# A recurrent layer's gate tiles moved behind its recurrences' inputs, its scans a tile ahead, its output in two halves, and two pairs of first tiles in turn

## The chip, the cores and the metric

The kernel runs on one NeuronCore of a Trainium2 chip. The metric is the device time of one execution in microseconds, as the median of several runs. All numbers of the profile come from one profiled execution; engines are named as the profile names them: PE (TensorE matmuls), PEld (its weight loads), DVE (VectorE), ACT (ScalarE), POOL (GpSimd), SP (SyncE).

## What is computed

Two blocks follow each other over one sequence of 512 tokens with 1024 features, all in fp32. The first block is a modulated mixer (state-space part and attention in parallel) and a feed-forward layer of 4096 features, `x + gate2 * (relu(h2 @ w_mlp1)**2 @ w_mlp2)`. The second block is a gated recurrent layer, then a causal latent attention with a gate, then a last norm. The change is in the recurrent layer and at two borders of stages:

```python
def rglru_layer(x, norm_g, w_in, conv_w, conv_b, w_rg, b_rg, w_ig, b_ig, lam, w_out):
    u = rms_norm_2(x, norm_g) @ w_in                 # w_in is 1024 x 2560
    xb, gate = u[..., :1280], u[..., 1280:]
    xb = causal_depthwise_conv(xb, conv_w, conv_b)   # width 4
    r = sigmoid(xblk @ w_rg + b_rg)                  # ten blocks of 128 x 128
    i = sigmoid(xblk @ w_ig + b_ig)
    log_a = -8.0 * r * softplus(-lam)
    a = exp(log_a)
    bterm = sqrt(-expm1(2.0 * log_a)) * (i * xb)
    _, hs = associative_scan(_lin_combine, (a, bterm), axis=1)
    return (hs * silu(gate)) @ w_out                 # w_out is 1280 x 1024
```

Its result is added to the stream x. The layer after it begins with two norms of the new x and projects it into the key-value and query latents.

## The kernel before

Activations lie with features on the 128 partitions and the 512 tokens along the free axis, so the stream is KT = 8 tiles of 128x512 (`x_stream`). Every big product is made in "feature tiles" of 128 output features: `feature_tile` (L1045) goes over blocks k of 128 input features, and each block takes three matmuls (`split_mm`, L1039, so L1041 to L1043), high times high, high times low, low times high, since every fp32 operand is split into a high and a low part. A tile over 1024 inputs is therefore 24 matmuls of 512 columns, the recurrent layer's output tile over 1280 inputs is 30.

The weights come as one stream in the order in which PE uses them, cut into slabs of four 128x128 blocks (256 KB). For each slab SP issues a load into a ring of four raw buffers, ACT writes the high part (`hi_upto`, L592 to L600, into a ring of seven), POOL subtracts to get the low part (`low`, L554), and PE waits for the low part (`weights`, L1031). ACT makes no slab by itself: `tile_in(name)` (L602) first converts up to six slabs (AHEAD) past the slab where the tile begins, and a slab's buffer is free when PE has done the last tile of the slab seven before. Since ACT's queue runs strictly in order, an ACT that waits for DVE converts nothing in the meantime.

`plan` (L105) writes down the order of all tiles by hand, and with it the order of the weights; `BANK_OF` (L196 to L205) gives each tile its PSUM bank in turn from a ring of banks that depends on the tile's kind, and `start` (L1023) lets PE wait until the bank's last tile has been read out ("evacuated").

The recurrent layer has RT = 10 tiles of 128 channels. `rnn_steps` (L87) gives the order that all engines follow. An "xb" tile n is the convolution's input: DVE scales it by the norm's factor in PSUM (`scale_tile`, L1949), ACT writes the first tap with the bias (`conv_first`, L846, the activation is L851), DVE adds three taps (L1972), ACT writes its high part (`conv_hi`, L858), and DVE the low part (L1985), the latter only after it has scaled the next xb tile. "gates" n, two steps later, is two tiles of three matmuls each ("rg" and "ig"), three tanhs and one exp on ACT (L866, L870, L873, L876) and two combining instructions on DVE (`gate_x`, L1989, and `decay`, L1996). After the gates of tiles 4 and 9 a detour works on five tiles at once: DVE's `halve` (L2023, with L1959 and L1965) and ACT's `roots` (L878, square roots L883) alternate, with a table load on ACT before the roots and one before the next tanh. A "gt" tile n is the gate: `scale_tile`, then `recurrence` (L1998: one tensor_scalar that adds 1 to the decay, L2000, and the scan, L2002), then `gate_y` (L2004), which needs ACT's tanh of the gate (L890), then ACT's `gate_hi` (L892, L895) and DVE's `y_low` (L2012, L2020). In the order of before, gt tiles 0 to 4 stand between the xb and gates tiles of steps 7 to 11, and gt tiles 5 to 9 follow at the end.

Then come eight output tiles "oa" of ten blocks each (L1356). DVE adds each to the stream (`add_to_stream`, L2050, the instruction is L2052), ACT writes the high part of the next input, DVE its low part.

Two other places are touched. The first matrix of the feed-forward layer ("m1", L1340) starts when the norm of the stream is written block by block (`norm_split`, L1547, low parts L1554). The last projection ("ob", L1492) starts while the last attention head is still being finished on DVE and ACT (L2201 to L2206, L978, `split_head`, L2171).

In the latent attention, the first gate tile ("gh", 0) is read out late by DVE (`gate2`, L2166, after `rope_key`); the four value tiles ("vh", 0, 0 to 3) follow it on PE, and their banks come from a ring of three (0, 1, 2).

## Time and profile before

| | us |
|---|---|
| median of 3 runs | 1716.84 |
| lowest, highest | 1707.63, 1719.45 |
| the profiled execution's own time | 1715.92 |
| its span in the profile | 1713.8 |
| PE busy | 1618.2 (94%) |
| DVE busy | 1013.9 (59%) |
| POOL busy | 774.3 (45%) |
| ACT busy | 738.9 (43%) |

The profiled execution took 2.1 us more than its span. Matmul records overlap: a record of 0.39 us stands for a matmul that starts 0.23 us after the last one, so the distance of two starts is what a matmul costs, and busy time is no measure of it. The granted clock over the whole span was 0.978.

### The profile page before, as it was taken

The page shows a single profiled execution, that of the slowest core. Times are in us where ns is not written, and L with a number is a line of the kernel's source. Part 1 is how long each engine was busy: PE and PEld are TensorE (multiplying, and loading weights), DVE is VectorE, ACT ScalarE, POOL GpSimd, SP SyncE. Part 2 cuts the span into 40 slices and gives each one's busy share as a digit, 9 for nine tenths or more (in the row PEclk, how much of TensorE's full clock was granted, in tenths as well). Part 3 has the DMA queues.
Part 4 walks back from the last instruction along what each step waited for, and adds up shares of the span by engine and source line. Part 5 has one row for each costly group of instructions (what it writes and reads, how often), then busy time and mean ns, then how long its engine had stood idle before and what let it go on. Part 6 is the DMA issues. An engine that isn't in the chain of part 4 may idle for free. (4 is left out here: it accounts for less than half of the span.)

```text
span 1713.8 us, 23817 instructions
## 1 busy us (share of the span) xinstructions
PE 1618.2 (94%) x8328; PEld 1335.5 (78%) x8328; DVE 1013.9 (59%) x1357; ACT 738.9 (43%) x1347; POOL 774.3 (45%) x546
## 2 busy tenths in 40 slices
PE   4899999999999899999989999999999699789987
PEld 4687888888878688887868888888888587667766
DVE  4778989888739698487241311112488813357662
ACT  2366656646633544323242333334476434323332
POOL 1235565656656510256634444445535354233423
PEclk9999999999999999999999999999999899889998
DMA  7233343434332200367423333333323233111212
GB/s 300 66 114 111 117 136 108 115 123 123 105 87 67 68 26 1 123 234 245 137 72 99 98 99 93 101 90 98 90 76 93 75 92 98 50 49 50 62 32 74
DMA packets 76245, 171.30 MB, mean 100 GB/s; under 512 B 8240, under 2 KB 8624, under 8 KB 72816
## 3 DMA queue, kind: packets, MB, share of 16 engines
q1 hardware_dynamic: 68832, 133.09, 26.6%
q10 hardware_dynamic: 7312, 36.83, 6.2%
q8 instruction: 67, 1.10, 0.3%
q14 instruction: 34, 0.28, 0.1%
HBM read 167.67 MB, written 2.23 MB: 99 GB/s over the span
## 5 line engine op out<-in xcount | busy, mean ns | idle before, releaser
L557 POOL TENSOR_TENSOR w_lo<-w_raw,w_hi 128x512 fp32r<-128x512 f32 x457 | 683.5, 1517 | 691.6 <-ACT w_hi L599 691.2
L1041 PE MATMUL bank<-a_hi,w_hi 128*128 128x512 f32 x1040 | 418.3, 402 | 18.2 <-DVE a_lo L1554 8.9
L1043 PE MATMUL bank<-a_hi,w_lo 128*128 128x512 f32 x1040 | 408.7, 393 | 0.0
L1042 PE MATMUL bank<-a_lo,w_hi 128*128 128x512 f32 x1040 | 408.5, 393 | 0.0
L599 ACT ACTIVATE w_hi<-w_raw 128x512 fp32r<-128x512 f32 x457 | 261.3, 619 | 147.4 <-PE bank L1043 123.7
L1041 PEld LDWEIGHTS bank<-a_hi,w_hi 128*128 128x128 f32 x1040 | 197.2, 190 | 69.8 <-issue 15.7
L1041 PE MATMUL bank<-b_hi,w_hi 128*128 128x512 f32 x600 | 237.7, 396 | 0.6 <-POOL w_lo L557 0.6
L1043 PE MATMUL bank<-b_hi,w_lo 128*128 128x512 f32 x600 | 235.8, 393 | 0.0
L1042 PE MATMUL bank<-b_lo,w_hi 128*128 128x512 f32 x600 | 235.8, 393 | 0.0
L1043 PEld LDWEIGHTS bank<-a_hi,w_lo 128*128 128x128 f32 x1040 | 197.3, 190 | 42.6
L1042 PEld LDWEIGHTS bank<-a_lo,w_hi 128*128 128x128 f32 x1040 | 197.5, 190 | 41.3 <-issue 1.9
L1041 PEld LDWEIGHTS bank<-b_hi,w_hi 128*128 128x128 f32 x600 | 114.2, 190 | 24.7 <-POOL w_lo L557 1.1
L1043 PEld LDWEIGHTS bank<-b_hi,w_lo 128*128 128x128 f32 x600 | 114.1, 190 | 24.5
L1042 PEld LDWEIGHTS bank<-b_lo,w_hi 128*128 128x128 f32 x600 | 114.1, 190 | 23.8
L1939 DVE SCALAR_TENSOR_TENSOR x_stream<-bank,small,x_stream 128x512 f32<-128x512 f32 x32 | 24.0, 750 | 140.4 <-PE bank L1043 140.4
L1932 DVE TENSOR_TENSOR tmp<-tmp 128x512 f32<-128x512 f32 x32 | 22.7, 708 | 123.6 <-ACT tmp L831 123.6
L697 ACT ACTIVATE M<-cs_rows,cs 128x128 f32<-128x128 f32 x256 | 78.0, 388 | 0.0
L1615 DVE SCALAR_TENSOR_TENSOR tmp<-bank,small,tmp 128x510 f32<-128x510 f32 (+1 forms) x96 | 71.9, 749 | 3.4
L511 POOL TENSOR_TENSOR square_sum<-square_sum,sq 128x512 f32<-128x512 f32 x31 | 40.1, 1294 | 63.5 <-ACT sq L611 63.5
L1530 DVE SCALAR_TENSOR_TENSOR ada_acc<-ada_piece,small,ada_acc 128x2048 f32<-128x2048 f32 x21 | 62.2, 2962 | 7.6 <-DMA ada_piece<-ada 6.2
L831 ACT ACTIVATE tmp<-bank 128x512 f32<-128x512 f32 x32 | 19.1, 598 | 101.3 <-PE bank L1043 101.3
L1262 PEld LDWEIGHTS bank<-v_and_ones,probs 128*128 128x128 f32 x512 | 60.2, 192 | 1.9 <-ACT gates_early L644 1.2
(327 smaller groups left out, 2460.9 us busy)
## 6 DMA issues: line engine op xcount, KB each, us to landing
w_raw<-ws SPq DMA_DIRECT2D x457, 256.0 KB, 2.7
cs_rows<-cs_scratch ACTq DMA_DIRECT2D x16, 1024.0 KB, 5.2
ada_piece<-ada ACTq DMA_DIRECT2D x16, 1024.0 KB, 5.3
ada_piece<-ada SPq DMA_DIRECT2D x8, 1024.0 KB, 15.0
x_stream<-x SPq DMA_DIRECT2D x1, 2048.0 KB, 15.9
x_stream<-x ACTq DMA_DIRECT2D x1, 2048.0 KB, 9.1
out<-x_stream SPq DMA_DIRECT2D x8, 256.0 KB, 2.1
rope_table<-rope ACTq DMA_DIRECT2D x1, 512.0 KB, 3.4
```

The costliest lines, as they stand in the source:

```text
L511: nc.gpsimd.tensor_tensor(sq_sum[:, :], first[:, :], sq[n % 2][:, :], ALU.add).then_inc(sq_added, 1)
L557: nc.gpsimd.tensor_tensor(wlo[b][:, :], raw[n % RAW_RING][:, :], r32(whi[b][:, :]), ALU.subtract)\
L599: A(whi[n % RING][:, :], raw[n % RAW_RING][:, :], ACT.Copy).then_inc(hi_done, 1)
L697: a(A(Dm[:, r, w], csB[:, r, w], ACT.Abs, bias=csT[:, c, h:h + 1]))
L1041: mm(out, lh, rh, start=first, stop=False)
L1042: mm(out, lh, rl, start=False, stop=False)
L1043: return mm(out, ll, rh, start=False, stop=last)
L1262: ins = mm(OQ[h % 2][:, i * W:(i + 1) * W], PT[:, c, i * P:(i + 1) * P], vv[:, c, h // 4, :], start=(c == 0 and i == 0), stop=(c == NCH - ...
L1530: V.scalar_tensor_tensor(into[:, :], src[:, :], csl[:, k:k + 1], into[:, :], ALU.mult, ALU.add).then_inc(ada_acc, 1)
L1615: ins = V.scalar_tensor_tensor(out[:, o], src[:, s], cwh[:, j * 24 + i:j * 24 + i + 1], out[:, o], ALU.mult, ALU.add)
L1932: v(V.tensor_tensor(full[:, :], r[:, :], r[:, :], ALU.mult))
L1939: inc_evac(V.scalar_tensor_tensor(xF[:, m, :], gb(name)[:, :], modc[:, 5 * KT + m:5 * KT + m + 1], xF[:, m, :], ALU.mult, ALU.add), name)
```

## The change

1. In `rnn_steps` all ten gt tiles stand behind the last gates tile; before, five of them stood between the xb and gates tiles. The weights' order follows.
2. DVE's addition of 1 to the decay goes to ACT: after each five square roots ACT runs five Identity activations with bias 1 (`a_full`).
3. The scan of tile n + 1 is issued before `gate_y(n)`, and writes over its own input; `y_low(n - 1)` is issued after `scale_tile` of tile n instead of right behind `gate_y(n - 1)`.
4. Each output tile is made in two halves of five blocks: first the first half of all eight tiles, each added to the stream, then the second half of all eight.
5. The first two tiles of m1 and of ob are made in turn, block by block (`tile_pair`), so that each arriving block feeds six matmuls instead of three.
6. The sixteen half tiles instead of eight shift all later banks; ("gh", 0) is restricted to banks 0 and 1.

```diff
@@ rnn_steps
     for n in range(RT + RNN_LAG):
-        if n >= RNN_HALF + RNN_LAG:
-            steps.append(("gt", n - RNN_HALF - RNN_LAG))
         if n < RT:
             steps.append(("xb", n))
         if n >= RNN_LAG:
             steps.append(("gates", n - RNN_LAG))
-    return steps + [("gt", n) for n in range(RT - RNN_HALF, RT)]
+    return steps + [("gt", n) for n in range(RT)]
@@ plan
-    for m in range(KT):
-        tile(("oa", m), RT)
+    for part in range(2):
+        for m in range(KT):
+            tile(("oa", part, m), RNN_HALF)
@@ banks
-        (0, 1, 2) if _name[0] in LATENT else (0, 1, 3, 5, 6) if _name[0] == "ob" else (0, 1, 3, 4, 5, 6)
+        (0, 1) if _name == ("gh", 0) else (0, 1, 2) if _name[0] in LATENT else (0, 1, 3, 5, 6) if _name[0] == "ob" else (0, 1, 3, 4, 5, 6)
@@ ScalarE
-            def roots(first):
-                for n in range(first, first + RNN_HALF):
+            def roots(first, count):
+                for n in range(first, first + count):
                     act.wait_ge(p_ready, n + 1)
                     if n >= 2:
                         act.wait_ge(xbs_done, n - 1)
                     A(root_v[n % 2][:, :], t[n % 2][:, :], ACT.Sqrt, scale=-0.25).then_inc(s_done, 1)
+                for n in range(first, first + count):
+                    A(t2[:, n, :], t2[:, n, :], ACT.Identity, bias=ones[:, 0:1]).then_inc(a_full, 1)
...
             for m in range(KT):
-                hi_upto(slab_of(("oa", m)) + AHEAD)
-                wait_evac(act, ("oa", m))
+                hi_upto(slab_of(("oa", 0, m)) + AHEAD)
+            for m in range(KT):
+                hi_upto(slab_of(("oa", 1, m)) + AHEAD)
+                wait_evac(act, ("oa", 1, m))
@@ TensorE
+            def tile_pair(names, hi, lo, ready):
+                for name in names:
+                    start(name)
+                blocks = TILES[names[0]][2]
+                for k, parts in enumerate(zip(*(weights(name) for name in names))):
+                    pe.wait_ge(*ready(k))
+                    for name, (b, o) in zip(names, parts):
+                        ins = split_mm(gb(name)[:, :], whi[b][:, o:o + P], wlo[b][:, o:o + P], hi(k), lo(k), k == 0,
+                                       k == blocks - 1)
+                        if k == blocks - 1:
+                            ins.then_inc(gemm_done, 1)
...
             for f in range(FQ):
-                for m in range(KT):
-                    feature_tile(("m1", f, m), in_a, in_a_lo, (rdyA, KT))
+                if f == 0:
+                    tile_pair((("m1", 0, 0), ("m1", 0, 1)), in_a, in_a_lo, lambda k: (rdyA, KT + k + 1))
+                for m in range(0 if f else 2, KT):
+                    feature_tile(("m1", f, m), in_a, in_a_lo)
...
-            for m in range(KT):
-                feature_tile(("oa", m), lambda k: bH[:, k, :] if k < KT else yH[k - KT][:, :],
-                             lambda k: bL[:, k, :] if k < KT else yL[k - KT][:, :],
-                             lambda k: (rdyB, 24 + KT * FQ + k + 1) if k < KT else (rdyY, k - KT + 1))
-                if m:
-                    stat("nkv", m - 1)
+            for part in range(2):
+                k0 = part * RNN_HALF
+                for m in range(KT):
+                    feature_tile(("oa", part, m), lambda k: in_y(k0 + k), lambda k: in_y_lo(k0 + k),
+                                 lambda k: (rdyB, 24 + KT * FQ + k0 + k + 1) if k0 + k < KT else (rdyY, k0 + k - KT + 1))
...
-            for m in range(KT):
-                feature_tile(("ob", m), in_a, in_a_lo, (rdyA, 4 * KT))
-                if m:
-                    stat("fin", m - 1)
+            tile_pair((("ob", 0), ("ob", 1)), in_a, in_a_lo, lambda k: (rdyA, 4 * KT + k + 1))
+            for m in range(2, KT):
+                feature_tile(("ob", m), in_a, in_a_lo)
+                stat("fin", m - 1)
@@ VectorE
             def recurrence(n):
                 ve.wait_ge(xbs_done, n + 1)
-                v(V.tensor_scalar(t2[:, n, :], t2[:, n, :], 1.0, None, ALU.add))
-                v.settle()
-                v(V.tensor_tensor_scan(scan[:, :], t2[:, n, :], xbi[:, n, :], 0.0, ALU.mult, ALU.add))
+                ve.wait_ge(a_full, n + 1)
+                v(V.tensor_tensor_scan(xbi[:, n, :], t2[:, n, :], xbi[:, n, :], 0.0, ALU.mult, ALU.add))
...
                 else:
+                    if n == 0:
+                        recurrence(n)
                     scale_tile(("gt", n), rstd, gt_scaled)
-                    recurrence(n)
+                    if n:
+                        y_low(n - 1)
+                    if n + 1 < RT:
+                        recurrence(n + 1)
                     gate_y(n)
-                    y_low(n)
+            y_low(RT - 1)
...
             for m in range(KT):
-                add_to_stream(("oa", m), m)
+                add_to_stream(("oa", 0, m), m)
+            for m in range(KT):
+                if m < 2:
+                    wait_evac(ve, ("oa", 0, m))
+                add_to_stream(("oa", 1, m), m)
                 if m:
-                    wait_evac(ve, ("oa", m - 1))
+                    wait_evac(ve, ("oa", 1, m - 1))
                     gain_low("nkv", m - 1, aL, aH, hiA, 3 * KT, rdyA)
```

## Rows read from the trace of the kernel before

**Rows 1.** stretch table: busy us (instructions) PE, PEld, DVE, ACT, POOL, then PEclk, DMA, GB/s

```profile
1340.00:1370.00 30.00, 20.44 (x76) 15.03 (x75) 23.91 (x27) 11.09 (x20) 13.33 (x10) 0.84 0.27 72
```

**Rows 2.** waits of PE: releaser: us in total, times, longest

```profile
PE bank L1041 <- DVE a_lo L1554: 8.9, 9, 3.1
PE bank L1041 <- DVE y_lo L2020: 7.5, 2, 5.3
PE bank L1041 <- POOL w_lo L557: 7.5, 6, 4.5
```

**Rows 3.** timeline of PE: start us, us, line, operation [idle before <- releaser]

```profile
1217.35 0.39 PE L1041 MATMUL bank<-a_hi,w_hi 128*128 128x512 f32 x1
...
1314.96 0.40 PE L1041 MATMUL bank<-xb_hi,w_hi 128*128 128x512 f32 x1
...
1337.57 0.47 PE L1041 MATMUL bank<-a_hi,w_hi 128*128 128x512 f32 x1 [4.46 <-POOL w_lo L557]
...
1352.13 0.39 PE L1041 MATMUL bank<-b_hi,w_hi 128*128 128x512 f32 x1
...
1367.17 0.80 PE L1041 MATMUL bank<-y_hi,w_hi 128*128 128x512 f32 x1 [5.31 <-DVE y_lo L2020]
```

**Rows 4.** timeline of DVE, same columns, the recurrent stage and its end

```profile
1276.54 0.69 DVE L1953 TENSOR_TENSOR bank<-bank,rstd 128x512 f32<-128x512 f32 x1
...
1337.74 1.22 DVE L2002 TENSOR_TENSOR_SCAN std<-tanh_half_log_a,gated_x 128x512 f32<-128x512 f32 x1
...
1341.01 0.69 DVE L2020 SCALAR_TENSOR_TENSOR b_lo<-y_full,b_hi 128x512 fp32r<-128x512 f32 x1 [0.69 <-ACT b_hi L895]
1341.73 0.70 DVE L1953 TENSOR_TENSOR bank<-bank,rstd 128x512 f32<-128x512 f32 x1
...
1343.17 2.20 DVE L2002 TENSOR_TENSOR_SCAN std<-tanh_half_log_a,gated_x 128x512 f32<-128x512 f32 x1
...
1348.10 0.70 DVE L1953 TENSOR_TENSOR bank<-bank,rstd 128x512 f32<-128x512 f32 x1
...
1418.82 0.69 DVE L2052 TENSOR_TENSOR x_stream<-x_stream,bank 128x512 f32<-128x512 f32 x1 [5.53 <-PE bank L1043]
```

**Rows 5.** timeline of ACT, same columns, the recurrent stage

```profile
1269.43 1.28 ACT L883 ACT_TABLE_LOAD   x1
...
1282.85 0.78 ACT L851 ACTIVATE xb_conv<-bank,params 128x512 f32<-128x512 f32 x1 [0.50 <-PE bank L1043]
...
1328.17 0.81 ACT L876 ACTIVATE tmp<-tmp,small 128x512 f32<-128x512 f32 x1
```

**Rows 6.** groups of instructions, 1217.3 to 1418.9 us: busy us, mean ns | idle before

```profile
L599 ACT ACTIVATE w_hi<-w_raw 128x512 fp32r<-128x512 f32 x64 | 36.5, 617 | 0.0
...
L1972 DVE SCALAR_TENSOR_TENSOR xb_conv<-bank,params,xb_conv 128x509 f32<-128x509 f32 (+2 forms) x30 | 22.4, 747 | 2.6 <-ACT xb_conv L851 1.9
...
L1989 DVE SCALAR_TENSOR_TENSOR gated_x<-tmp,xb_conv 128x512 f32<-128x512 f32 x10 | 12.0, 1198 | 4.1 <-ACT tmp L870 4.1
...
L873 ACT ACTIVATE tanh_half_log_a<-tmp,small 128x512 f32<-128x512 f32 x10 | 8.1, 814 | 0.0
...
L866 ACT ACTIVATE tmp<-bank,small 128x512 f32<-128x512 f32 x10 | 6.8, 677 | 0.0
```

**Rows 7.** timeline of PE at the starts of m1 and of ob

```profile
864.35 0.77 PE L1041 MATMUL bank<-a_hi,w_hi 128*128 128x512 f32 x1 [2.47 <-DVE a_lo L1554]
...
874.62 0.40 PE L1041 MATMUL bank<-a_hi,w_hi 128*128 128x512 f32 x1
...
880.07 0.39 PE L1041 MATMUL bank<-a_hi,w_hi 128*128 128x512 f32 x1
...
1655.44 0.69 PE L1041 MATMUL bank<-a_hi,w_hi 128*128 128x512 f32 x1
...
1662.29 0.50 PE L1041 MATMUL bank<-a_hi,w_hi 128*128 128x512 f32 x1 [1.58 <-DVE a_lo L2171]
```

**Rows 8.** timeline of PE at the third value tile

```profile
1483.50 0.80 PE L1041 MATMUL bank<-w_hi,ckv_hi 128*128 128x512 f32 x1 [7.29 <-DVE tmp L2166]
```

More of the change, by code:

```diff
@@ L36 @@
 RNN_HALF = RT // 2
+ROOTS_AT = {RNN_HALF - 1: (0, RNN_HALF), RT - 1: (RNN_HALF, RT - RNN_HALF)}
 CKT, CQT = KV_RANK // P, Q_RANK // P
@@ L361, in build @@
             sil = [sb(f"gate_silu{b}", [P, SEQ]) for b in range(2)]
-            scan, yF = std, sb("y_full", [P, SEQ])
+            yF = sb("y_full", [P, SEQ])
         with Arena():
@@ L425, in build @@
         xb_scaled, gt_scaled = sem("xb_scaled"), sem("gt_scaled")
-        p_ready, a_exp, am1_done = sem("decay_variance"), sem("decay"), sem("decay_minus_one")
+        p_ready, a_exp, am1_done, a_full = (sem(n) for n in ("decay_variance", "decay", "decay_minus_one", "decay_full"))
         g_th, y2_ready = sem("gate_tanh"), sem("y2_ready")
@@ L518, in _ @@
                 for m in range(1, POOLED[norm]):
-                    tile = (kind, FQ - 1, m) if kind == "m2" else (kind, m)
+                    tile = (kind, FQ - 1, m) if kind == "m2" else (kind, 1, m) if kind == "oa" else (kind, m)
                     squares.setdefault(min((TILES[tile][1] + TILES[tile][2] - 1) // BPS + RING, N_SLABS), []).append((norm, m))
@@ L906, in _ @@
                         conv_hi(n + RNN_LAG)
-                    if n % RNN_HALF == RNN_HALF - 1:
-                        roots(n + 1 - RNN_HALF)
+                    if n in ROOTS_AT:
+                        roots(*ROOTS_AT[n])
                 else:
@@ L1355, in _, with in_y, in_y_lo @@
                     feature_tile((kind, n), in_a, in_a_lo)
-            for m in range(KT):
-                feature_tile(("oa", m), lambda k: bH[:, k, :] if k < KT else yH[k - KT][:, :],
-                             lambda k: bL[:, k, :] if k < KT else yL[k - KT][:, :],
-                             lambda k: (rdyB, 24 + KT * FQ + k + 1) if k < KT else (rdyY, k - KT + 1))
-                if m:
-                    stat("nkv", m - 1)
+            def in_y(k):
+                return bH[:, k, :] if k < KT else yH[k - KT][:, :]
+            def in_y_lo(k):
+                return bL[:, k, :] if k < KT else yL[k - KT][:, :]
+            for part in range(2):
[3 more added lines that the diff above has]
+                                 lambda k: (rdyB, 24 + KT * FQ + k0 + k + 1) if k0 + k < KT else (rdyY, k0 + k - KT + 1))
             pe.wait_ge(rows_kept, 2)
@@ L2009, in gate_y @@
                 v.settle()
-                V.tensor_tensor(yF[:, :], scan[:, :], th[:, :], ALU.mult).then_inc(y2_ready, 1)
+                V.tensor_tensor(yF[:, :], xbi[:, n, :], th[:, :], ALU.mult).then_inc(y2_ready, 1)
             def y_low(n):
@@ L2021, in y_low, with scale_inputs @@
                 ve.wait_ge(rdy, r0 + 1)
-            def halve(first):
+            def scale_inputs(first, count):
                 variance(first)
                 variance(first + 1)
-                for n in range(first, first + RNN_HALF):
+                for n in range(first, first + count):
                     scale_x(n)
-                    if n + 2 < first + RNN_HALF:
+                    if n + 2 < first + count:
                         variance(n + 2)
@@ L2041, in _ @@
                         conv_low(RT - 1)
-                    if n % RNN_HALF == RNN_HALF - 1:
-                        halve(n + 1 - RNN_HALF)
-                else:
+                    if n in ROOTS_AT:
+                        scale_inputs(*ROOTS_AT[n])
+                else:
+                    if n == 0:
+                        recurrence(n)
                     scale_tile(("gt", n), rstd, gt_scaled)
-                    recurrence(n)
+                    if n:
+                        y_low(n - 1)
+                    if n + 1 < RT:
+                        recurrence(n + 1)
                     gate_y(n)
-                    y_low(n)
+            y_low(RT - 1)
             def add_to_stream(name, m):
```

4 lines of the change are left out of this document (2 added, 2 removed).

## The prediction

> **What bounds the kernel now.** I read the page first: PE is busy 94% of the span, so a gain can only be time in which PE stands still or runs at the lower clock. Then the waits of PE: the three lines that the change can touch are 8.9 us on low parts of a norm, 7.5 on the recurrent layer's last low parts and 7.5 on weights [rows 2]. Then PE's timeline for the price of work: a tile of 24 matmuls takes 880.07 - 874.62 = 5.45 us, 0.227 a matmul [rows 7]. With it the recurrent stage splits into three stretches [rows 3]:
>
> - xb, gates and five gt tiles, 1217.35 to 1316.3 (the last gates tile starts at 1314.96 and takes 1.4): 99.0 us for 420 matmuls, which cost 95.3. The other 3.7 are mostly the small matmuls of the norm.
> - the five last gt tiles, to 1352.13: 35.8 us for 120 matmuls (27.2). 8.6 are lost, 4.46 of it in one wait for weights: ACT had not yet turned to converting.
> - the output, to 1418.8 (DVE's last addition starts there [rows 4]): 66.7 us for 240 matmuls (54.5). 12.2 are lost, 5.31 of it in one wait for the low part of y.
>
> So PE runs ahead of an ACT/DVE chain: PE has made gates 9 at 1316.3, ACT ends its exp at 1329.0 [rows 5]. A stall also costs clock: from 1340 to 1370 the granted clock is 0.84, between the levels 1.2 and 2.4 GHz [rows 1]. 16% of 30 us is 4.8 us, idle time included; I take 1.6 us for one long stall.
>
> **1. Stretch without gt tiles.** For PE 300 matmuls remain: 68.1 + 3.7 us, so it could start gt 0 at 1289.2. The chain decides otherwise. Up to the five-tile detour behind gates 4 nothing changes; DVE comes out of it at 1276.5 [rows 4], ACT 0.7 earlier, at 1275.8. New there: five Identity activations. The trace has none in this place; the bounds are the 0.57 us of a slab conversion (36.5 / 64) and the 0.81 of a tanh with a bias [rows 6]; I take 0.66, nearer to the conversion since the source is also in SBUF: 3.3 us (2.9 to 4.1), on the path. Then conv_first 7 starts at 1279.1 instead of 1282.85 [rows 5], because gt 0 no longer stands in front of it. One step of the chain: conv_first 0.7, two slabs 1.1, three tanhs and an exp, whose records of 0.68 and 0.81 overlap by 0.1, 2.6, DVE's decay 0.7, the next scaling 0.6 [rows 6], some 0.2 for handovers: 5.9 us, against 6.8 on PE (30 matmuls). The first step also takes the table load for tanh, 1.28 [rows 5]: 7.2. So conv_first 9 comes at 1292.2, the low part that gates 9 needs one step later, at 1298.1, and gates 9 is done at 1299.5, with some slow matmuls 1300.0. PE stands for 10.8 us that it did not stand before (between 0 and 15: that is the chain hidden wholly, or each step 1.4 longer). DVE's additions of 1 (L2000) leave the chain, but were in it only with the gt tiles.
>
> **2. Gate tiles.** At gates 9 ACT has converted six slabs ahead, which is gt 0 to 2: 16.3 us, to 1316.3. ACT ends the exp of gates 9 about 3.3 us after PE, at 1303.3; the detour takes the same 7.1 us as the first one (1269.43 to 1276.54 [rows 4, 5]), its roots end at 1309.7, the five Identities at 1313.0. The next slab is there with its low part 2.0 later, at 1315.0: no stall, with 1.3 us to spare. A second table load and tanh 0 (1.9), then DVE's two gate instructions (0.69 each, as the additions [rows 4]): y 0 is ready at 1317.0, and the two slabs behind it at 1319.6 and later, where PE wants the first at 1319.0: 0.6 us of stall.
> From there one tile costs DVE and ACT now 1348.10 - 1341.73 = 6.37 us [rows 4], more than PE's 5.45, and this is why PE ran dry. Two things leave this cycle: L2000 (1343.17 - 1341.73 - 0.61 for the scaling = 0.83) and the wait of y_low for ACT, 0.69 [rows 4], since the next scaling covers it; the tanh is covered by the scan ahead. 4.84 remain, under 5.45, so PE sets the pace. Gate tiles end at 1300.0 + 54.5 + 0.6 + 1.6 of clock = 1356.7.
>
> **3. Output.** y 9 follows within some 4 us and is wanted first by the second half, 8 x 15 matmuls (27.2 us) later. No wait is left: 240 matmuls at 0.229 (tile borders) are 55.0, to 1411.7. The halves add eight additions to DVE, 8 x 0.69 = 5.5 us, under PE: DVE idles 5.53 between two of them [rows 4], and a half tile takes 3.4; without that cover they would cost 5.5. ACT's conversions of the first half are all queued before its first waiting copy, so no slab hangs on DVE. POOL's sum of squares comes at twice the pace; I take 0 for it (up to 1.3, one sum at the end, below nothing excluded).
> Gain of the stage: 1418.8 - 1411.7 = 7.1.
>
> **4. First tiles in turn.** m1: blocks arrive every 1.45 us; the first tile took 864.35 to 874.62, the second ended at 880.07 [rows 7]. Six matmuls are 1.36 us, about the arrival's pace, and the first few run slow: 864.35 + 8 x 1.36 + 1.6 = 876.8. Gain 3.2 (0 if its weights are late; 4.9 if only the last block bounds it). Four slabs are needed at once; nothing holds ACT and POOL from having made six before the norm. ob: the last block was waited for at 1662.29 [rows 7], two tiles would end at 1668.4. In turn it is wanted at 1655.44 + 42 x 0.227 = 1665, when it is there: end 1666.6, gain 1.8 (0 to 1.8).
>
> **5. Banks.** PE waits 7.29 us for DVE to read out the first latent gate [rows 8]. This is the third value tile, since it takes gh 0's bank. Counting the new bank list, gh 0 sits in bank 1 and the second value tile takes it: the same release, six more matmuls behind it. 1.4 us at full clock, 2.6 at the lower one; I take 2.0 lost. The other latent tiles keep their distance of three in the ring.
>
> **Sum.** 7.1 + 3.2 + 1.8 - 2.0 = 10.1 us. The profiled execution took 1715.92, so 1705.8; the median of before, 1716.84, is only 0.9 above it.
>
> **Rivals.**
> A: the chain is hidden, PE reaches gt 0 at its own pace. For it: a step of the chain, 5.9, is shorter than PE's 6.8. Against: the chain starts the race at 1279.1, when xb 7, by PE's pace from 1264, is already some 8 us old. Then 1289.2 + 54.5 + 55.0 = 1398.7, 20.1 gained, with the rest 23.1: 1692.8.
> B: weights starve the gate tiles, slower than before. ACT converts two slabs only after each y, so PE follows the DVE/ACT cycle wherever that is over 5.45. Evidence: the scan took 2.20 us in one tile and 1.22 in another [rows 4], gated_x 1.20 in the mean [rows 6] where an instruction of its size takes 0.75, so DVE is sometimes held up. If the reordering saves nothing and y_low doubles, the cycle is 7.07; with y 0 2.4 us later, y 9 is at 1383.0, the slab of the fifth half tile 2.6 later, 15 slabs (40.8) and the clock behind it: 1428.0, 9.2 lost, in sum 6.2 slower: 1722.1. It turns the gain of the whole into a loss from a cycle of about 6.4.
> The Trainium skill, "SBUF — State Buffer", section "Who interferes with whom", says that a VectorE instruction with two SBUF inputs contends with a GpSimd one that reads SBUF, and that the loser is blocked for the whole instruction. By that rule y_low, the scan and the product are all exposed to POOL's low parts, which is B's mechanism; the trace agrees for the scan, with 2.20 against 1.22.
> C: the pairs do nothing, since their second tiles' weights are late. For it: 7.5 us of waits for weights exist [rows 2]; against: none stands at these two places. 5.0 less gain: 1710.8.
>
> **How the numbers follow.** Forecast 0.70, A 0.15, B 0.07, C 0.08. A measurement of this kernel tells about 1% (17 us) from no change. My 10.1 us are 0.6%: "same". Faster by over 1% needs 17.2 us: A, and a tail of the forecast (a chain 7 us shorter than I think), 0.18 together. Slower by over 1% needs more than B: 0.04. The range goes from A's time less 1.8 to near B's: 1691 to 1720.
>
> **What would show it.** Right: gt 0 starts on PE near 1300; a gap of some 10 us before it, in two or three waits for xb_lo (L1985), which were none; no wait of over 1 us among the gate tiles; the 4.46 and 5.31 waits gone; a step from gate tile to gate tile of 5.45 on PE; the stage ends near 1411.7 counted from an unchanged start, less the 3.2 of m1; the wait at the value tile is at the second one. Wrong: PE waits for w_lo among the gate tiles (B), or no wait before gates 9 (A), or waits for w_lo in the pairs (C).

## The result, and the profile after

The changed kernel takes 1704.1 us (median of 10 runs, 1698.4 to 1710.9), the kernel before 1716.9 in the runs beside it: ratio 0.9933, 95% interval 0.9912 to 0.9955. The prediction was 1705.8.

The profiled execution was the longest of the ten, 1710.9 us with a span of 1709.0. Cut at six places, the two spans compare so:

| stretch of the span, us | before | after | difference | predicted |
|---|---|---|---|---|
| to the first matmul of m1 | 864.35 | 870.09 | +5.7 | 0 |
| from there to the first xb matmul | 353.00 | 350.61 | -2.4 | -3.2 |
| recurrent stage: to the start of DVE's last addition to the stream | 201.47 | 193.30 | -8.2 | -7.1 |
| to the first latent score | 84.19 | 84.49 | +0.3 | +2.0 |
| to the first ob matmul | 152.43 | 154.55 | +2.1 | 0 |
| to the end | 58.36 | 55.96 | -2.4 | -1.8 |

The first line holds no changed instruction; in the twelve experiments below it took 863.6 to 867.7 us. The fifth took 151.4 to 152.8 in eight of them and 154.5 to 155.4 in the other four. So 7.8 us of this execution lie where nothing of the change is seen at work; without them it would be 1703.1, close to the median.

PE's waits in the stage, in its timeline (start, duration, line, operation, [idle before <- releaser]). They answer to [rows 3]:

```profile
1220.70 0.39 PE L1044 MATMUL bank<-a_hi,w_hi 128*128 128x512 f32 x1
...
1281.31 0.47 PE L1044 MATMUL bank<-xb_hi,w_hi 128*128 128x512 f32 x1 [0.58 <-DVE xb_lo L2009]
...
1285.31 0.50 PE L1044 MATMUL bank<-a_hi,w_hi 128*128 128x512 f32 x1 [2.37 <-DVE xb_conv L1996]
...
1295.94 0.77 PE L1044 MATMUL bank<-xb_hi,w_hi 128*128 128x512 f32 x1 [3.29 <-DVE xb_lo L2009]
...
1301.21 0.76 PE L1044 MATMUL bank<-xb_hi,w_hi 128*128 128x512 f32 x1 [2.37 <-DVE xb_lo L2009]
...
1303.91 0.63 PE L1044 MATMUL bank<-a_hi,w_hi 128*128 128x512 f32 x1
...
1358.95 0.39 PE L1044 MATMUL bank<-b_hi,w_hi 128*128 128x512 f32 x1
```

All idle time now stands before the last gates tile: four waits, 8.6 us. The gate tiles (1303.9 to 1358.95, ten of 5.5 us) and the output run without one. The waits of 4.46 and 5.31 us of before are gone. PE's waits over the whole span (us in total, times, longest), beside [rows 2]:

```profile
PE bank L1044 <- DVE tmp L2198: 10.6, 1, 10.6
PE bank L1044 <- DVE a_lo L1578: 7.1, 5, 3.2
PE bank L1044 <- DVE xb_lo L2009: 6.2, 3, 3.3
...
PE bank L1044 <- DVE xb_conv L1996: 2.4, 1, 2.4
...
PE bank L1044 <- POOL w_lo L556: 0.5, 1, 0.5
```

The waits for a norm's low parts fell from nine to five (8.9 to 7.1 us), those for weights from 7.5 to 0.5, those for y's low parts from 7.5 to none. One wait grew: 10.6 us at the value tiles, where it was 7.3 [rows 8].

ACT's timeline around the two detours, beside [rows 5]; x5 is five instructions in one record:

```profile
1279.08 3.16 ACT L884 ACTIVATE tanh_half_log_a<-tanh_half_log_a,consts 128x512 f32<-128x512 f32 x5
1282.14 0.76 ACT L850 ACTIVATE xb_conv<-bank,params 128x512 f32<-128x512 f32 x1
...
1312.68 3.16 ACT L884 ACTIVATE tanh_half_log_a<-tanh_half_log_a,consts 128x512 f32<-128x512 f32 x5
1315.75 0.62 ACT L598 ACTIVATE w_hi<-w_raw 128x512 fp32r<-128x512 f32 x1
```

Five additions of 1 take 3.16 us, and conv_first of xb 7 starts right behind them; in the second detour the next slab does. DVE's timeline over one gate tile, beside [rows 4], and POOL's two conversions in it:

```profile
1319.64 0.69 DVE L1977 TENSOR_TENSOR bank<-bank,rstd 128x512 f32<-128x512 f32 x1
1320.42 0.69 DVE L2043 SCALAR_TENSOR_TENSOR b_lo<-y_full,b_hi 128x512 fp32r<-128x512 f32 x1
1321.15 2.21 DVE L2025 TENSOR_TENSOR_SCAN gated_x<-tanh_half_log_a,gated_x 128x512 f32<-128x512 f32 x1
1323.29 0.66 DVE L2030 SCALAR_TENSOR_TENSOR gate_silu<-gate_silu,bank 128x512 f32<-128x512 f32 x1
1323.98 1.02 DVE L2033 TENSOR_TENSOR y_full<-gated_x,gate_silu 128x512 f32<-128x512 f32 x1
1324.92 0.69 DVE L1977 TENSOR_TENSOR bank<-bank,rstd 128x512 f32<-128x512 f32 x1
```

```profile
1320.99 1.29 POOL L556 TENSOR_TENSOR w_lo<-w_raw,w_hi 128x512 fp32r<-128x512 f32 x1 [3.26 <-ACT w_hi L598]
1322.24 2.20 POOL L556 TENSOR_TENSOR w_lo<-w_raw,w_hi 128x512 fp32r<-128x512 f32 x1
```

From scaling to scaling 5.28 us, without a gap that names a releaser. Before it was 6.37. The two engines stretch each other: the scan takes 2.21 us here and 1.22 alone, and POOL's second subtraction 2.20 where the first takes 1.29.

The pairs on PE, beside [rows 7], and the value tile, beside [rows 8]:

```profile
870.09 0.76 PE L1044 MATMUL bank<-a_hi,w_hi 128*128 128x512 f32 x1 [2.48 <-DVE a_lo L1578]
...
875.26 0.39 PE L1044 MATMUL bank<-a_hi,w_hi 128*128 128x512 f32 x1
...
883.42 0.39 PE L1044 MATMUL bank<-a_hi,w_hi 128*128 128x512 f32 x1
...
1477.59 0.80 PE L1044 MATMUL bank<-w_hi,ckv_hi 128*128 128x512 f32 x1 [10.56 <-DVE tmp L2198]
...
1498.49 0.30 PE L1448 MATMUL bank<-knope_hi,qnope_hi 128*128 128x128 f32 x1 [3.14 <-DVE qnope_lo L2176]
...
1653.04 0.69 PE L1044 MATMUL bank<-a_hi,w_hi 128*128 128x512 f32 x1
```

The third tile of m1 starts 13.3 us after the first instead of 15.7, with no wait inside; the first twelve matmuls, to 875.26, go at 0.43 us each, so at the lower clock of 1.2 GHz.

### The profile page after: what moved, and what is told of

Its sections match the earlier page's. It is cut to its first block, busy times and chain, and to the rows that moved or that the text cites. A ratio compares the mean times of both kernels' runs of the same rounds, so it can differ in the third digit from the quotient of the medians.

```text
span 1709.0 us, 23860 instructions
## 1 busy us (share of the span) xinstructions
PE 1620.6 (95%) x8328; PEld 1341.9 (79%) x8328; DVE 1024.2 (60%) x1355; ACT 744.7 (44%) x1357; POOL 780.5 (46%) x546
## 4 chain that ended last, share of the span: by engine, by line
PE 80%; DVE 14%; ACT 3%; issue 2%; DMA 1%; SPq 0%; ACTq 0%; DVEq 0%; POOL 0%
PE bank L1044 21%; PE bank L1046 21%; PE bank L1045 21%; PE bank L1279 3%; DVE ada_acc L1554 2%; PE bank L1090 2%; DVE rstd L1792 2%; PE bank L1477 1%; PE bank L1214 1%; DVE tmp L1639 1%; DMA x_stream<-x 1%; PE bank L1222 1%; PE bank L1270 1%; PE bank L1128 1%; PE bank L1271 1%
```

## The experiments

Each kernel was timed beside the kernel before on the same chip; a ratio is to that kernel. The experiments were timed in groups (e1 to e4, e5 to e8, e9 and e10, e11 and e12), with 4 to 10 runs each, and the kernel before had medians of 1716.0 to 1717.5 us beside them, so kernels of two groups are compared by their ratios. "Stage" is the third stretch of the table, "to the score" the fourth.

| kernel | median, us | ratio to before, 95% | stage | to the score |
|---|---|---|---|---|
| changed kernel | 1704.1 | 0.9933 [0.9912, 0.9955] | 193.3 | 84.5 |
| e1: tiles in the old order | 1704.1 | 0.9921 [0.9897, 0.9946] | 192.9 | 85.1 |
| e2: output in whole tiles | 1710.8 | 0.9957 [0.9943, 0.9971] | 196.2 | 83.6 |
| e3: additions of 1 on DVE | 1710.1 | 0.9966 [0.9949, 0.9984] | 198.5 | 85.0 |
| e4: before plus the pairs | 1710.7 | 0.9962 [0.9944, 0.9979] | 201.4 | 84.1 |
| e9: DVE in the old order | 1705.6 | 0.9946 [0.9923, 0.9968] | 192.8 | 83.5 |
| e5: first latent gate in bank 6 | 1698.2 | 0.9904 [0.9887, 0.9921] | 192.9 | 77.3 |
| e6: additions spread | 1704.8 | 0.9938 [0.9924, 0.9952] | 191.6 | 85.0 |
| e7: e6, gate tile 0 early | 1700.9 | 0.9914 [0.9900, 0.9928] | 191.3 | 83.3 |
| e8: e7 and e5 | 1694.7 | 0.9877 [0.9861, 0.9892] | 190.7 | 74.9 |
| e10: e6 and e5 | 1698.6 | 0.9903 [0.9879, 0.9928] | 192.6 | 78.8 |
| e11: e10, banks shifted as in e8 | 1697.2 | 0.9881 [0.9861, 0.9901] | 192.0 | 76.5 |
| e12: e8 without the spreading | 1695.5 | 0.9869 [0.9849, 0.9889] | 194.0 | 75.0 |

**e1, the order of the tiles.** Five gate tiles go back between the xb and gates tiles; the rest of the change stays.

```diff
     for n in range(RT + RNN_LAG):
+        if n >= RNN_HALF + RNN_LAG:
+            steps.append(("gt", n - RNN_HALF - RNN_LAG))
...
-    return steps + [("gt", n) for n in range(RT)]
+    return steps + [("gt", n) for n in range(RT - RNN_HALF, RT)]
...
-                    if n == 0:
+                    if n % RNN_HALF == 0:
                         recurrence(n)
...
-                    if n + 1 < RT:
+                    if (n + 1) % RNN_HALF:
                         recurrence(n + 1)
```

> The changed kernel with the old order of tiles only (gate tiles 0 to 4 again between the xb and gates tiles; additions of 1 on ACT, scans ahead within each five, halves, pairs stay). The stage is counted from the first xb matmul to DVE's last output addition: 201.5 us before, 193.3 after. Theory 1 (the order moved PE's idle time in front of gates 9 and is itself a loss; the gain comes from the shorter gate cycle and the halves): an ACT/DVE step with a gate tile is 11.8 less 1.5, under PE's 12.3, so the chain no longer lags, PE has gate tiles to fill the detour, and the stage is 181 to 187 us, 6 to 12 us shorter than in the changed kernel; no wait for xb_lo before gates 7 to 9. Theory 2 (the order is the source of the gain): the chain still lags and the last gate tiles starve, the stage is 193 to 202 us with waits for w_lo among gate tiles 5 to 9.

Moving the gate tiles back is worth nothing that can be measured here: 192.9 us of stage against 193.3. Neither theory fits as a whole. The 181 to 187 us of theory 1 did not come, and neither did its shorter step: two steps with a gate tile take 23.9 us from scan to scan (1290.18 to 1314.06), and 23.7 before (1289.95 to 1313.62). Theory 2 has the waits for weights right, but the order is not the source of the gain. PE no longer stands still before the gates, and waits for weights instead, in two waits of 2.10 and 5.83 us. The second one on PE, and ACT ahead of it:

```profile
1340.85 0.76 PE L1046 MATMUL bank<-a_hi,w_hi 128*128 128x512 f32 x1 [5.83 <-POOL w_lo L558]
```

```profile
1326.07 0.67 ACT L867 ACTIVATE tmp<-bank,small 128x512 f32<-128x512 f32 x1
...
1335.17 3.16 ACT L886 ACTIVATE tanh_half_log_a<-tanh_half_log_a,consts 128x512 f32<-128x512 f32 x5
1338.23 0.61 ACT L600 ACTIVATE w_hi<-w_raw 128x512 fp32r<-128x512 f32 x1
```

ACT reaches gates 9 at 1326.1 and converts its first slab for the late gate tiles at 1338.2, since the detour with its five additions is 3.16 us longer than before. Either order leaves 8 us idle: 8.6 in four waits, or 7.9 in two. The move only chooses where PE waits for the chain.

**e2, the output in whole tiles.**

```diff
-    for part in range(2):
-        for m in range(KT):
-            tile(("oa", part, m), RNN_HALF)
+    for m in range(KT):
+        tile(("oa", 1, m), RT)
```

> The changed kernel with whole output tiles of ten blocks. Theory 1: the last low part of y came at 1367.7 us, PE would want it 6.1 us after its last gate tile, at 1364.2: one wait of about 3.5 us for y_lo and up to 2 us of lower clock, the stage 196.8 to 199 us instead of 193.3. Theory 2 (without the starving of the gate tiles y is early enough, the halves do nothing): 193 to 194 us, no wait for y_lo.

The wait for the low part of y is back, and it is shorter than the 5.31 us of before, since y 9 itself comes earlier:

```profile
1365.41 0.50 PE L1041 MATMUL bank<-y_hi,w_hi 128*128 128x512 f32 x1 [2.47 <-DVE y_lo L2040]
```

The halves are worth 2.9 us of the stage, almost all of it this wait. That is theory 1, with a wait 1 us shorter than expected and the stage, at 196.2, just under its range. The ratio rises by 0.0024, which is 4.1 us; what the 1.2 us beyond the stage are is open, and the intervals overlap.

**e3, the additions of 1 back on DVE.**

```diff
-                for n in range(first, first + count):
-                    A(t2[:, n, :], t2[:, n, :], ACT.Identity, bias=ones[:, 0:1]).then_inc(a_full, 1)
...
-                ve.wait_ge(a_full, n + 1)
+                v(V.tensor_scalar(t2[:, n, :], t2[:, n, :], 1.0, None, ALU.add))
+                v.settle()
```

> The changed kernel with the additions of 1 back on DVE in front of each scan, ACT's ten Identity activations gone. Theory 1: the five Identities (3.16 us) lie on the chain in front of xb 7, so gt 0 starts 3.2 us earlier on PE (79.7 instead of 82.9 us after the first xb matmul); the gate cycle grows from 5.28 to 5.7 to 6.1 us, over PE's 5.45, but starts 6.3 us ahead, so that it is about even: stage 190 to 194 us. Theory 2 (moving them off DVE is what lets PE set the pace): the cycle is back at 6.2 or more and weights starve PE, stage 197 us or more with waits for w_lo.

The largest single part: the stage grows by 5.2 us. The gate tiles fall back to a step of 6.36 us, as theory 2 has it, and PE waits seven times for weights, five times among the gate tiles and twice at the first tiles of the output. DVE, POOL and PE in that kernel:

```profile
1320.27 1.42 DVE L2022 TENSOR_SCALAR tanh_half_log_a<-tanh_half_log_a 128x512 f32<-128x512 f32 x1
1321.72 2.19 DVE L2024 TENSOR_TENSOR_SCAN gated_x<-tanh_half_log_a,gated_x 128x512 f32<-128x512 f32 x1
```

```profile
1320.11 1.29 POOL L556 TENSOR_TENSOR w_lo<-w_raw,w_hi 128x512 fp32r<-128x512 f32 x1 [3.65 <-ACT w_hi L598]
1321.36 1.47 POOL L556 TENSOR_TENSOR w_lo<-w_raw,w_hi 128x512 fp32r<-128x512 f32 x1
```

```profile
1334.18 0.50 PE L1042 MATMUL bank<-a_hi,w_hi 128*128 128x512 f32 x1 [0.61 <-POOL w_lo L556]
```

And taking the five Identities out of the first detour started gates 9 only 1.5 us earlier (79.05 us after the stage's start instead of 80.51), not 3.2: of the four waits only the bank's went from 2.37 to 0.91.

**e4, the pairs alone**, on the kernel before.

```diff
+                if f == 0:
+                    tile_pair((("m1", 0, 0), ("m1", 0, 1)), in_a, in_a_lo, lambda k: (rdyA, KT + k + 1))
+                for m in range(0 if f else 2, KT):
+                    feature_tile(("m1", f, m), in_a, in_a_lo)
...
+            tile_pair((("ob", 0), ("ob", 1)), in_a, in_a_lo, lambda k: (rdyA, 4 * KT + k + 1))
+            for m in range(2, KT):
```

> The kernel before with the two pairs of first tiles only. Theory 1: m1's first two tiles take 13.3 us instead of 15.7 and ob's stage is 1.7 to 2.4 us shorter, 4.1 to 4.8 us in all, ratio 0.9972 to 0.9976; the recurrent stage stays at 201.5 us. Theory 2 (the pairs only move the stall to weights): ratio 1.000.

m1 gains 3.4 us (349.6 instead of 353.0), ob 2.4. The stage is as before, 201.4. So theory 1 holds, with 5.8 us where 4.1 to 4.8 were expected. By its ratio the pairs alone are worth some 6.5 us of the 11.5 of the whole change.

**e9, DVE's order of before**, with the additions on ACT.

```diff
-                    if n == 0:
-                        recurrence(n)
                     scale_tile(("gt", n), rstd, gt_scaled)
-                    if n:
-                        y_low(n - 1)
-                    if n + 1 < RT:
-                        recurrence(n + 1)
+                    recurrence(n)
                     gate_y(n)
-            y_low(RT - 1)
+                    y_low(n)
```

> The changed kernel with DVE's order of before in the gate tiles: the scan of tile n behind the scaling of tile n, its low part right behind its product; the additions of 1 stay on ACT. Theory 1, the reordering is a part of what brought DVE's cycle under PE's step of 5.45 us: the low part waits again for ACT's high part, some 0.6 us per tile, so that the cycle of 5.28 us becomes 5.8 to 6.1, PE follows it, and the stage of 193.3 us grows by 2 to 5 us; time 1706 to 1709. Theory 2, with the addition of 1 gone from DVE the cycle stays under 5.45 in either order (0.69 for the missing handover is all there is, and the scan runs beside less of POOL's work in the old order): the stage stays within 0.7 us of 193.3, time 1703 to 1705.5.

No difference: the stage is 192.8. DVE and POOL over one gate tile:

```profile
1315.60 0.70 DVE L1977 TENSOR_TENSOR bank<-bank,rstd 128x512 f32<-128x512 f32 x1
1316.20 1.61 DVE L2025 TENSOR_TENSOR_SCAN gated_x<-tanh_half_log_a,gated_x 128x512 f32<-128x512 f32 x1
...
1320.15 0.69 DVE L2043 SCALAR_TENSOR_TENSOR b_lo<-y_full,b_hi 128x512 fp32r<-128x512 f32 x1 [0.70 <-ACT b_hi L896]
1320.88 0.70 DVE L1977 TENSOR_TENSOR bank<-bank,rstd 128x512 f32<-128x512 f32 x1
```

```profile
1315.44 3.46 POOL L556 TENSOR_TENSOR w_lo<-w_raw,w_hi 128x512 fp32r<-128x512 f32 x2 [3.26 <-ACT w_hi L598]
```

The wait of 0.70 for ACT is back as expected, yet the step is 5.28 us again: the scan is 0.6 shorter. With the additions on DVE the two orders agree as well: 6.37 in the kernel before, 6.36 in e3. What two orders have in common is the distance from the start of POOL's first subtraction to the end of the scan's record: 1321.15 + 2.21 - 1320.99 = 2.37 us with the scan ahead, 1316.20 + 1.61 - 1315.44 = 2.37 in the old order. With the additions on DVE it is 3.80 in e3 (1321.72 + 2.19 - 1320.11) and 3.80 in the kernel before, where POOL's record starts at 1341.57 and the scan's is in [rows 4]. So the scan's end hangs on POOL, POOL on ACT's conversion, that on ACT's high part of y, and that on the product behind the scan. This loop sets the step of DVE.

The two distances can be built from the rows. Alone, a subtraction of POOL takes 1.29 us, the addition of 1 takes 0.42 and the scan 1.22. Where one of these starts while the other engine's instruction runs, it ends its lone duration after the other's end, less 0.13 to 0.21 us. In e3 the first subtraction ends at 1321.40 and the addition at 1321.69, the second subtraction at 1322.83, the scan at 1323.91: 1.29 + 0.42 + 1.29 + 1.22 less three times 0.14 is 3.80. Without the addition the scan itself starts beside the first subtraction, in both orders: 1.29 + 1.22 - 0.14 = 2.37. Taking the addition away takes a whole subtraction out of the loop with it, 3.80 - 2.37 = 1.43 us; less the 0.33 by which the product is now longer (1.02, since it meets the second subtraction) this is the 1.1 that the step fell by. Once the first subtraction has started it makes no difference how early the scan is issued, so where `scale_tile` and `y_low` stand between is free. The loop is read from the rows of four kernels; no run changed POOL's work.

**e5, the first latent gate tile in bank 6**, which the value tiles do not use.

```diff
-        (0, 1) if _name == ("gh", 0) else (0, 1, 2) if _name[0] in LATENT else ...
+        (6,) if _name == ("gh", 0) else (0, 1, 2) if _name[0] in LATENT else ...
```

> The changed kernel with one edit: the first latent gate tile gets bank 6, which is not in the ring of the value tiles, so that no value tile has to wait until DVE has read the gate tile out. In the changed kernel the second value tile waited 10.56 us for that. Theory 1, the wait is for the bank alone: no wait of over 1 us stands at the value tiles, and the distance from the stream's last addition to the first score, 84.5 us in the changed kernel, shrinks by 7 to 11 us, to 74 to 78; the time is 1693 to 1697 us, ratio to the changed kernel's 1704.1 about 0.994 to 0.996. Theory 2, DVE's chain of norms, rotated keys and splits bounds the first scores anyway: the value wait goes, but a wait of the same length stands at the first scores or behind them, the distance stays at 83 to 85 and the time at 1702 to 1706.

The wait was for the bank: the time falls to 1698.2 us, 1 us above the range of theory 1, and the distance to the score by 7.2. The same edit made on two other kernels, e6 to e10 and e7 to e8, lowers the ratio by 0.0035 and 0.0037, some 6 us each. Not all of the 10.6 us are won, because ACT is next. PE at the value tiles of e5, then ACT:

```profile
1467.20 0.79 PE L1044 MATMUL bank<-w_hi,ckv_hi 128*128 128x512 f32 x1 [3.84 <-ACT v_tok L965]
```

```profile
1463.74 1.28 ACT L959 ACT_TABLE_LOAD   x1 [1.41 <-DVE bank L1977]
1465.03 0.60 ACT L959 ACTIVATE tmp<-bank 128x512 f32<-128x512 f32 x1
1465.52 1.14 ACT L598 ACTIVATE w_hi<-w_raw 128x512 fp32r<-128x512 f32 x2
1466.56 1.56 ACT L965 ACTIVATE v_tok<-bank 128x512 f32<-128x512 f32 x3
```

ACT reads the first value tile out behind a table load, the gate's activation and two slabs, all of it behind DVE's scaling of the gate tile.

**e6, the additions of 1 spread over the gate tiles** instead of standing at the end of a detour.

```diff
-                for n in range(first, first + count):
-                    A(t2[:, n, :], t2[:, n, :], ACT.Identity, bias=ones[:, 0:1]).then_inc(a_full, 1)
+            def add_one(n):
+                A(t2[:, n, :], t2[:, n, :], ACT.Identity, bias=ones[:, 0:1]).then_inc(a_full, 1)
...
+                    if n == 0:
+                        add_one(0)
+                        add_one(1)
...
+                    if n + 2 < RT:
+                        add_one(n + 2)
```

> The changed kernel with ACT's additions of 1 taken out of the end of each detour: nothing else changes. Additions 0 and 1 stand before the first gate tanh, addition n + 2 behind the tanh of gate tile n. The decision is on the first detour: five Identities take 3.16 us there, and stand before the first scaled copy of xb 7. Theory 1, these 3.16 us are on the path to the last gates tile, and the second detour's likewise on the path to the first y: gates 9 starts on PE 1.5 to 3.2 us earlier than 80.5 us after the stage's start, the stage (first xb matmul to the stream's last addition, 193.3 in the changed kernel) takes 190 to 192, the time is 1701 to 1703. Theory 2, the xb tiles wait for their banks and for DVE's order instead (the kernel with the additions on DVE won only 1.5 us there): gates 9 moves by under 1 us and the stage stays at 192.5 to 194; or the scans now wait for their additions and weights run short, 194 or more.

Gates 9 starts at 79.07, so 1.4 us earlier, and the profiled stage is 1.7 shorter. The time, 1704.8, does not show it: its ratio, 0.9938, is not below the changed kernel's 0.9933. So theory 1 has the stage right and the time not.

**e7, gate tile 0 early**, on top of e6: on PE it stands between gates 7 and gates 8, in a bank of its own.

```diff
+PE_STEPS = [s for s in RNN_STEPS if s != ("gt", 0)]
+PE_STEPS.insert(PE_STEPS.index(("gates", 8)), ("gt", 0))
...
-    _b = _ring[_turn % len(_ring)]
+    _b = 7 if _name == ("gt", 0) else _ring[_turn % len(_ring)]
...
-    _turn += 1
+    _turn += _name != ("gt", 0)
...
+                        hi_upto(slab_of(("gt", 1)) + AHEAD)
```

> As the kernel with the additions of 1 spread, and on PE gate tile 0 is made between the gates tiles 7 and 8, in a bank of its own, while DVE and ACT read it out in the old place; ACT converts one tile's slabs more before the first gate tanh. PE stood still for 8.6 us in four waits of the stretch before the last gates tile, 5.7 of them in two waits for xb's low part. Theory 1, that idle time is left by the chain and can be filled with work that hangs on nothing: the waits before gates 8 and 9 shrink by 4 to 5.5 us in sum, the last gates tile is not later by over 1 us, and the stage is 4 to 5 us shorter than with the additions spread alone (185 to 188 us; time 1696 to 1699). Theory 2, the gain is given back at the gate tiles, where ACT has to come out of the second detour before it converts: PE now reaches the slabs 5 us sooner and waits that much for weights, stage 190 to 193.

The wait of 3.3 us before gates 8 is filled, and the gain is given back nearly in full, as theory 2 has it:

```profile
1321.28 0.79 PE L1053 MATMUL bank<-a_hi,w_hi 128*128 128x512 f32 x1 [4.18 <-POOL w_lo L558]
```

The stage is 191.3 against 191.6. The time is nevertheless 3.9 us lower than e6's. The edit also moved every later tile by one bank: instead of one wait of 10.6 us the value tiles now have two, of 3.2 and 6.3, and the distance to the score is 83.3 us against e6's 85.0.

**e8, e7 and e5 together.** It has the lowest median of all, 1694.7 us. Of the four cases that were laid out it is the second, only the bank: the stage, 190.7, stays well above 185 to 188, and the distance to the score, 74.9, is in its range.

> The kernel with gate tile 0 early and the additions spread, and with the first latent gate tile in bank 6 as well. If both ideas hold and add up: stage 185 to 188 and last addition to first score 74 to 78, time 1686 to 1692. If only the bank holds: 1693 to 1697; if only the stage: 1696 to 1699; if neither: 1702 to 1706.

**e10 to e12, what the early tile is worth beside the shifted banks.** e10 is e6 and e5 together. e11 adds to it only the two lines that give gate tile 0 bank 7 and no turn of the ring; the tile stays in its place. e12 is e8 with the additions again at the end of each detour.

> The changed kernel with two edits that were run alone before: ACT's additions of 1 spread over the gate tiles (the stage 191.6 instead of 193.3 us), and the first latent gate tile in bank 6 (last addition to first score 77.3 instead of 84.5 us). Gate tile 0 stays in its place. If the early gate tile 0 only moved a wait (it made four us of it among the gate tiles) and what it won besides came from the banks that it shifted, this kernel has a stage of 191 to 192 us and 77 to 78 us to the first score, in sum 1695.5 to 1698; if the early tile helped by itself, the kernel with all three (1694.65) stays ahead by 2 us or more; if the two edits add up fully and the early tile was worth nothing, 1693 to 1695.

> The kernel with the additions of 1 spread and the first latent gate tile in bank 6, and one more edit: gate tile 0 of the recurrent layer has bank 7 to itself and takes no turn of the ring, so that every later tile has the bank of the kernel with the early gate tile (1694.65 us), while gate tile 0 stays in its old place on PE. Theory 1, the 3.9 us between that kernel and the one without the early tile came from the shifted banks (the value tiles' ring then starts at bank 2, and the second value tile waits 3.2 us for the rotated key's bank instead of 3.8 for ACT's copy): last addition to first score 74.5 to 75.5 us instead of 77.3 to 78.8, time 1693 to 1696. Theory 2, they came from the early tile: 77 to 79 us there if the banks do nothing, time 1697.5 to 1700. Half and half: the time between, 1695.5 to 1697.5, the distance at 75 and the stage at 191.6 to 192.6.

> The kernel with all three edits (1694.65 us) without the spreading: the additions of 1 stand at the end of each detour again, gate tile 0 is early and in bank 7, the first latent gate tile is in bank 6. Theory 1, spreading is worth nothing by itself (1704.8 against 1704.1 and 1698.6 against 1698.15 us in two pairs): 1694 to 1696. Theory 2, the early tile needs it, since ACT comes out of the second detour 1.9 us later and the wait for weights among the gate tiles (4.2 us) grows to 5.5 to 6: stage 192 to 193.5, time 1696 to 1699.

By the ratios, e10 is level with e5 (0.9903 and 0.9904), and e11, e12 and e8 are level among themselves (0.9881, 0.9869, 0.9877). The shift of the banks alone takes e10 to 0.9881, some 3.8 us, and the early tile adds some 0.7 to that (both are differences of ratios, times 1717). The intervals of e10 and e11 overlap, so that the shift carries most of it is likely and not settled (by the medians, 1698.6 and 1697.2, it is 1.3 us); e11's distance to the score, 76.5, also stands between the two theories. What the shift does shows in PE's wait at the value tiles of e11, 3.21 us for the rotated key's bank in place of 3.83 for ACT in e10:

```profile
1461.37 0.50 PE L1050 MATMUL bank<-w_hi,ckv_hi 128*128 128x512 f32 x1 [3.21 <-DVE tmp L2120]
```

The spreading is worth nothing: e12 without it is no slower, though its wait for weights is longer (5.2 us) and its profiled stage 194.0.

## Why the prediction was right, and where it was not

The total was right within 1.7 us, and no stretch but the untouched ones is off by more than that. Some of it is offsetting, and some is luck: ten runs scatter from 1698.4 to 1710.9 us, and the profiled one is 5.1 us above the prediction because the untouched stretches took 7.8 more.

**Stretch without gate tiles: right.** Gate tile 0 was expected 82.65 us after the stage's start and came at 1303.91 - 1220.70 = 83.21. Five Identities were put at 3.3 us and took 3.16. PE was to lose 10.8 us there and lost 11.4 (83.21 less 68.1 and 3.7): 8.6 in waits, and 2.7 because the twelve matmuls of gates 8 and 9, behind the two longest waits for xb's low part, start 0.42 to 0.57 us apart instead of 0.23. Two or three waits for xb's low part were forecast and three came. The wait of 2.37 us for xb_conv, which is one for a bank, was not foreseen, and e3 and e6 show that a shorter detour moves the last gates tile by 1.4 us and not by the detour's 3.2. The prediction had put all five Identities on the path; less than half of them is. What holds the rest is not shown: the waits before gates 8 and 9 stay as they were.

**Gate cycle: the direction right, the reason half wrong.** The step was to fall from 6.37 to 4.84 by two removals, 0.83 for the addition and 0.69 for the wait of `y_low`. It fell to 5.28, and e9 shows that the reordering gives none of it. The failing step is "two things leave this cycle". Only the addition was in the loop that sets the step; the wait of `y_low` was not. And the durations of DVE's instructions were added as if they were fixed, but they stretch with what POOL does beside them: the scan takes 2.21 us here and 1.61 in e9, against 1.22 alone [rows 4]. The addition alone is worth 1.08 (6.36 in e3 less 5.28), more than its own 0.83, because a subtraction of POOL leaves the loop with it. PE's 5.45 is still above 5.28 by 0.17 us a tile, so the pace was PE's, as forecast; the margin is less than a third of the 0.61 that was counted on.

**Gate tiles and output.** The ten gate tiles took 1358.95 - 1303.91 = 55.0 us, where 56.7 were expected (54.5, a stall of 0.6 and 1.6 of clock): the stall did not come, and only the first few matmuls were slow. The output took 1414.00 - 1358.95 = 55.05 against 55.0; 1414.00 is the start of DVE's last addition.

**The order of the tiles.** The prediction added up the stage as a whole, and never asked what the old tile order would do with the other edits in place. e1 answers: the same. The gain of the stage comes from the additions on ACT (5.2 us by e3) and the halves (2.9 by e2), together 8.0 of the 8.2 that were measured; the order and the scans ahead give nothing by themselves. Each was taken out of the changed kernel alone. Whether two of them together would cost more than their sum was not run.

**The pairs: right.** 3.2 and 1.8 were expected. The profile of the changed kernel has 2.4 and 2.4, e4 has 3.4 and 2.4. The first term varies by 1 us between executions with the point at which the clock rises: behind about seven slow matmuls in e4, behind twelve in the changed kernel.

**Banks: the size off.** The wait moved to the second value tile as forecast. The 2.0 us lost were 0.3. Behind the release there are 20.90 us to the score instead of 19.51, which is the 1.4 of six matmuls at full clock. The distance ahead of the release shrank by 1.1 us, which the prediction had left at zero. More important, the prediction treated a wait of 7.3 us as given, and e5 shows that some 6 us of it, 10.6 by then, were a matter of one bank's number.

**Rivals.** A (the chain hidden) is out by the 8.6 us of waits. B (weights starve the gate tiles) is out in the changed kernel, which has no such wait there, but its mechanism is real: e3 has it at a step of 6.36 us, and it costs seven waits of about 0.6 us each and 5.2 us of stage. Two of B's numbers do not hold. Its cycle of 7.07 us looks like 6.37 plus the doubled `y_low`, and so keeps the addition that the change takes off DVE. And a cycle of about 6.4 was to turn the gain into a loss, but e3, at 6.36, is still faster than the kernel before (0.9966, interval to 0.9984). C (the pairs do nothing) is out by e4.

## What to carry to other kernels

When two engines wait for each other in every round, sum the loop that closes through both and not one engine's instructions: here the removal of one instruction inside the loop gave 1.1 us a tile, more than the instruction took, and a reordering outside it nothing. Filling an idle stretch of the bounding engine gives nothing if a later wait hangs on the same chain; the early gate tile won 3.3 us before the gates and lost 4.2 behind them. And before work is moved about, look at the longest wait for a buffer: a different bank for one tile, one edited number, won some 6 us, as much as the two pairs.

## What was not expected of the hardware

- An instruction of DVE is stretched by POOL's subtraction beside it, and not the scan alone. In e3 adding 1 takes 1.42 us when POOL's subtraction starts 0.16 before it, and 0.42 in the same kernel when POOL is idle:

```profile
1308.96 0.42 DVE L2022 TENSOR_SCALAR tanh_half_log_a<-tanh_half_log_a 128x512 f32<-128x512 f32 x1
```

  The Trainium skill, "SBUF — State Buffer", section "Who interferes with whom", says that `tensor_scalar` in a two-port mode and instructions with two SBUF inputs both want the pair of ports that GpSimd uses, and that whoever issues second is blocked until the first is done. The trace agrees but for a remainder. In e3 the addition starts 0.16 us behind a subtraction of 1.29, and the scan 0.36 behind one of 1.47. Blocked to the end of the subtraction, they would take 1.29 - 0.16 + 0.42 = 1.55 and 1.47 - 0.36 + 1.22 = 2.33; they take 1.42 and 2.19, 0.13 and 0.14 less. It holds the other way round too: the second subtraction of the changed kernel starts 1.12 us before the scan's end and takes 2.20 instead of 1.29, where 1.12 + 1.29 would be 2.41.
- The stretch behind the first latent score has the lower clock for a time that differs from execution to execution, with the same waits in it. Two pieces of it differ, and each begins behind a wait that is equally long in both traces (3.14 and 1.72 us). The stretch table (busy us of PE, PEld, DVE, ACT, POOL, then the granted clock, DMA, GB/s), first of the changed kernel, then of e6:

```profile
1498.49:1520.50 22.01, 20.09 (x85) 15.67 (x85) 5.82 (x12) 4.72 (x10) 7.23 (x7) 0.77 0.17 48
1638.54:1650.23 11.69, 10.94 (x52) 7.55 (x53) 6.36 (x8) 2.33 (x5) 1.35 (x2) 0.85 0.00 0
```

```profile
1491.56:1512.16 20.60, 18.67 (x85) 14.40 (x85) 5.82 (x12) 4.72 (x10) 7.21 (x7) 0.83 0.16 52
1630.27:1640.32 10.05, 9.30 (x52) 6.86 (x53) 6.37 (x8) 2.34 (x5) 1.35 (x2) 1.00 0.00 0
```

  With the same number of matmuls the first piece is 1.4 us longer in the changed kernel and the second 1.6, together the 3.0 by which the whole stretch differs. In e8 the first piece takes even 24.45 us, at a granted clock of 0.67. So one profile can be 2 to 3 us off here with no difference in the work.
